# Two-block transformer kernel: the first norm's squares made between the copies of x and added by VectorE

## The reference, cut to what matters

```python
def rms_norm(x, gain):
    xf = x.astype(jnp.float32)
    xf = xf * lax.rsqrt(jnp.mean(xf * xf, axis=-1, keepdims=True) + NORM_EPS)
    return (xf * gain.astype(jnp.float32)).astype(x.dtype)
...
for l in range(DEPTH):                       # DEPTH = 2
    h = rms_norm(x, norm_mix[l])
    proj = h @ w_in[l]                       # 1024 -> 5120 columns
    ...                                      # two attentions, gates, output projection
    x = x + mixed @ w_out[l]
    h = rms_norm(x, norm_ffn[l])
    x = x + conv_ffn(h, w_up[l], conv_w[l], conv_b[l], w_down[l])
return rms_norm(x, norm_final)
```

## Time and profile before

| | |
|---|---|
| median of 3 runs | 1078.23 us (1077.58 to 1080.33) |
| the profiled execution | 1077.55 us, its span 1075.5 us |
| TensorE busy | 1057.4 us, 98% of the span |
| VectorE / ScalarE / GpSimd busy | 717.1 / 572.3 / 289.2 us |
| mean granted clock of TensorE | 0.996 |

### The profile page before, as it was taken

One profiled execution on the slowest core, in us unless ns is written; L12 is line 12 of the kernel. 1 busy time (PEld: TensorE's weight loads), 2 busy tenths in 40 slices (PEclk: granted clock), 3 DMA queues, 4 the chain that ended last, 5 costly groups with the idle time before them and its releaser, 6 DMA issues.

```text
span 1075.5 us, 20022 instructions
## 1 busy us (share of the span) xinstructions
PE 1057.4 (98%) x8402; PEld 1004.7 (93%) x8402; DVE 717.1 (67%) x1209; ACT 572.3 (53%) x789; POOL 289.2 (27%) x186
## 2 busy tenths in 40 slices
PE   7999999999999999999999999999999999999997
PEld 6999998999899899999999989998999999999996
DVE  3772228788678766322688867877887789666663
ACT  4545356564355553653756544556557865343442
POOL 2176675300000127566750000003300034101020
PEclk9899999999999999999999999999999999999999
DMA  8454444555664575344455557537333157564751
GB/s 293 157 184 131 157 155 159 165 188 170 218 197 142 182 230 178 105 150 157 134 182 195 187 170 230 167 123 212 116 113 118 60 177 225 172 212 130 242 176 39
DMA packets 169689, 180.11 MB, mean 167 GB/s; under 512 B 4224, under 2 KB 166400, under 8 KB 169472
## 3 DMA queue, kind: packets, MB, share of 16 engines
q1 hardware_dynamic: 169600, 178.84, 51.8%
HBM read 177.78 MB, written 1.05 MB: 166 GB/s over the span
## 4 chain that ended last, share of the span: by engine, by line
PE 90%; DVE 3%; ACT 3%; POOL 2%; issue 1%; DMA 1%; SPq 0%; DVEq 0%; POOLq 0%; ACTq 0%
PE psum L669 89%; ACT sb_scratch L1311 1%; DVE sb_w_lo L1824 1%; DMA sb_raw<-in_w_in 1%; ACT sb_w_hi L1311 1%; POOL sb_w_lo L2565 1%; POOL sb_rs L2581 1%; PE psum L888 1%; DVE psum L1815 0%; DVE sb_xg_lo L1815 0%; ACT sb_xg_hi L1311 0%; POOL sb_scratch L2603 0%; ACT sb_sq L1311 0%; DVE sb_scratch L1815 0%; ACT L1311 0%
## 5 line engine op out<-in xcount | busy, mean ns | idle before, releaser
L669 PE MATMUL psum<-sb_xg_hi,sb_w_hi 128*128 128x256 f32 x1656 | 411.3, 286 | 1.0 <-DVE sb_xg_lo L1815 1.0
L1311 ACT ACTIVATE sb_w_hi<-sb_raw 128x2048 fp32r<-128x2048 f32 (+3 forms) x185 | 318.1, 1724 | 176.7 <-PE psum L669 113.2
L669 PE MATMUL psum<-sb_xg_lo,sb_w_hi 128*128 128x256 f32 x1656 | 406.2, 283 | 0.0
L1824 DVE TENSOR_TENSOR sb_w_lo<-sb_raw,sb_w_hi 128x2048 fp32r<-128x2048 f32 (+3 forms) x151 | 307.1, 2037 | 114.7 <-ACT sb_w_hi L1311 113.9
L669 PEld LDWEIGHTS psum<-sb_xg_hi,sb_w_hi 128*128 128x128 f32 x1656 | 316.9, 191 | 4.0 <-DVE sb_xg_lo L1815 1.5
L669 PEld LDWEIGHTS psum<-sb_xg_lo,sb_w_hi 128*128 128x128 f32 x1656 | 317.4, 192 | 0.3
L669 PE MATMUL psum<-sb_xg_hi,sb_w_lo 128*128 128x256 f32 x1656 | 234.6, 285 | 0.7 <-DVE sb_w_lo L1824 0.7
L669 PEld LDWEIGHTS psum<-sb_xg_hi,sb_w_lo 128*128 128x128 f32 x1656 | 214.5, 192 | 1.6 <-DVE sb_w_lo L1824 0.9
L669 PE MATMUL psum<-sb_hid_both,sb_w_hi 128*128 128x512 f32 (+1 forms) x912 | 210.4, 364 | 1.2 <-DVE sb_hid_both L1899 1.2
L2565 POOL TENSOR_TENSOR sb_w_lo<-sb_raw,sb_w_hi 128x2048 fp32r<-128x2048 f32 (+1 forms) x34 | 156.1, 4597 | 111.1 <-ACT sb_w_hi L1311 101.2
L669 PEld LDWEIGHTS psum<-sb_hid_both,sb_w_hi 128*128 128x128 f32 x912 | 150.4, 190 | 22.6 <-DVE sb_hid_both L1899 2.5
(11 more groups left out here) (168 smaller groups left out, 997.1 us busy)
## 6 DMA issues: line engine op xcount, KB each, us to landing
sb_raw<-in_w_in SPq DMA_DIRECT2D x52, 1024.0 KB, 5.2
sb_raw<-in_w_up SPq DMA_DIRECT2D x44, 1024.0 KB, 5.1
sb_raw<-in_w_ff SPq DMA_DIRECT2D x21, 1024.0 KB, 5.8
sb_raw<-in_w_down SPq DMA_DIRECT2D x16, 768.0 KB, 4.8
sb_raw<-in_w_down SPq DMA_DIRECT2D x16, 640.0 KB, 4.4
sb_raw<-in_w_out SPq DMA_DIRECT2D x8, 1024.0 KB, 5.2
sb_raw<-in_w_ff SPq DMA_DIRECT2D x8, 768.0 KB, 4.5
sb_raw<-in_w_ff SPq DMA_DIRECT2D x8, 640.0 KB, 4.5
```

Of the source, the lines that this page charges most:

```text
L669: return nc.tensor.matmul(ps, lhsT, rhs, start=start, stop=stop, skip_group_check=True)
L1311: return nc.scalar.activation(out_, in_, func, **kw)
L1824: v.tensor_tensor(part(w_lo, s), part(raw, s), part(w_hi, s).bitcast(F32), ALU.subtract)\
```

## The change

ScalarE makes the squares of tiles 0 to 3 right behind the fourth `xg_full`, before the fifth, and those of tiles 4 to 7 at the old place. `sq` now has four buffers for them (`m % 4`). The additions move from GpSimd to VectorE: three of them behind the copies of x tiles 4, 5 and 6, the other four behind the low half of slab 1 and ahead of the low half of slab 2. ScalarE's split of slab 2 stays behind the last square. The counts of the semaphores are kept in step.

```diff
+            def first_square(m):
+                f(tl(sq, m % 4), tl(xt, m), ACT.Square).then_inc(S["square"], 1)
...
                 f(tl(xg_full, m), tl(xt, m), ACT.Copy, scale=col("norm_mix0", m)).then_inc(S["xg_full"], q.one("xg_full"))
+                if m == 3:
+                    for i in range(4):
+                        first_square(i)
                 if m == 4:
                     split(1)
...
-            for m in range(KD):
-                q.next("x_tile")
-                square_room(m)
-                f(tl(sq, m % 2), tl(xt, m), ACT.Square).then_inc(S["square"], 1)
+            for m in range(4, KD):
+                act.wait_ge(S["sq_added"], max(m - 4, 1))
+                first_square(m)
+            q.next("x_tile", KD)
+            q.next("sq_added", KD - 1)
+            q.next("stat_sum")
             split(2)
...
+            def add_square(m):
+                dve.wait_ge(S["square"], m + 1)
+                if m > 1:
+                    dve.wait_ge(S["sq_added"], m - 1)
+                v.tensor_tensor(SUMS[0], tl(sq, 0) if m == 1 else SUMS[0], tl(sq, m % 4), ALU.add).then_inc(S["sq_added"], 1)
...
             for m in range(KD):
                 if q.due("x_turned", m + 1):
                     dve.wait_ge(S["x_turned"], m + 1)
                 v.tensor_copy(tl(xt, m), turned(m)).then_inc(S["x_tile"], 1)
+                if 4 <= m < 7:
+                    add_square(m - 3)
...
             split(1)
+            for m in range(4, KD):
+                add_square(m)
             split(2)
...
-            add_squares()
+            q.next("square", KD)
+            q.next("stat_sum")
+            q.sent["sq_added"] = KD - 1
```

## The result

The changed kernel takes 1071.84 us, the median of 4 runs (1071.60 to 1072.89), against 1078.10 us for the kernel before. The ratio is 0.9938, with a 95% interval of 0.9922 to 0.9954. Five more runs on another occasion gave 1072.10 against 1078.20 us and 0.9944 [0.9931, 0.9958]; one execution of the kernel before took 5334.77 us there and is left out of the ratio. The prediction was 1071.8 us.

What follows compares the result with a forecast made beforehand. TensorE, busy 98% of the span, was taken to bound the kernel. Pause 4.4 plus clock 2.0 minus 0.2 us at slab 8 gave 6.2 us gained: 1071.8 us, own range 1070.8 to 1072.8, wider range 1070.5 to 1074.2.

Steps and rivals of the forecast that it cites:

- The pause, 4.4 us: TensorE's wait ahead of the first norm's stat() goes: stat() at 23.7 us against 28.09, 4.4 us gained.
- The clock, 2.0 us: TensorE's matmuls from 28.09 to 32.53 us, run at 1.2 GHz, would keep 2.4 GHz: 2.0 us gained.
- full clock: Profile reading that TensorE, busy 352.41 of 353.00 us from 30 to 383 us, ran at 2.4 GHz throughout.
- Squares and early additions at nothing: In the opening, ScalarE's first four squares (1.33 us) and VectorE's first three additions (0.45 us each) fit idle time: no cost.
- a sign of being wrong: In the profile after, a copy of x later than before would count against the prediction.
- The late additions, 1.8 us: VectorE's last four additions behind slab 1's low half, one every 0.45 us, complete the sum at 23.6 to 23.7 us.
- at the same moment: The sum of squares is ready just when TensorE, done with 8 low matmuls, could start stat(), at 23.71 us.
- Slab 2: ScalarE splits it at 20.3 us instead of 26.66, VectorE's low half runs 23.65 to 25.9: 1.1 us of slack for TensorE.
- Minus 0.2 us at slab 8: Other engines gain 4.95 us against TensorE's 6.4; 1.4 us less slack makes VectorE 0.2 us late for TensorE's sb_b.
- the short pause that stays: Rival: additions before stat() at GpSimd's pace leave a 1.6 us pause; gain 4.6 us, 1073.6 us, chance 0.10.
- the thin slack at slab 8: Rival: slack elsewhere is thinner than read, TensorE takes on all of 1.4 us; gain 5.0 us, 1073.2 us, chance 0.06.
- the first rival: Additions before stat() slow, one every 0.87 us, four in 3.5 us: a 1.6 us pause, 1073.6 us, chance 0.10.

Runs made afterwards that it cites:

- fill_pause: Kernel before with 32 extra matmuls on TensorE ahead of stat(), inside its pause, into an unused bank; 1076.34 us, ratio 0.9987.
- more_turns: Changed kernel with 22 instead of 16 idle turns on TensorE before x has landed; 1073.55 us, ratio 0.9950.
- hold_slab2: Changed kernel, but ScalarE waits for stat() before it splits slab 2; 1075.39 us, ratio 0.9971.
- pad_vector: Changed kernel with four extra dependent additions on VectorE behind the low half of slab 2, result unused; 1073.03 us, ratio 0.9957.
- low_first: Changed kernel with VectorE's low half of slab 2 ahead of the last four additions instead of behind them; 1075.68 us, ratio 0.9979.
- late_squares: Changed kernel with all eight squares back behind the xg_hi tiles and all seven additions on VectorE behind slab 1's low half; 1074.47 us, ratio 0.9964.
- gpsimd_adds: Changed kernel with all seven additions back on GpSimd, squares still early and in four buffers; 1075.98 us, ratio 0.9981.

## Why the prediction was right, step by step

- **The pause, 4.4 us.** 5.34 us from the low pass to `stat()` became 0.96: 4.38 us. Against the second profile of the kernel before it is 4.49 - 0.96 = 3.5 us. fill_pause, which keeps the pause and only its clock, was 4.2 us slower than the changed kernel (1076.34 - 1072.10), so the split between pause and clock holds in the medians too.
- **The clock, 2.0 us.** 4.44 us became 2.34: 2.1 us. In the second profile of the kernel before it was 1.4 us by the same rows, and against fill_pause it is 1.7 and 1.0. So 2.0 us lies near the upper end of what the profiles show. The prediction's "full clock" over the window from 30 to 383 us is a rounded mean: its first 2.5 us were at half, which changes 1.00 by less than 0.004.
- **Squares and early additions at nothing.** 1.32 us for four squares (1.33 was said), 0.69 us of ScalarE's idle time left behind them and 0.33 us left between the copies. In the first profile x was copied later than before, which the prediction had named as a sign of being wrong; the rows above show neither in its way, and the twelve low passes are no later with them.
- **The late additions, 1.8 us.** They took 2.01 us; a dependent addition comes every 0.53 us, not 0.45. It cost nothing, since TensorE came later to `stat()` in all three profiles of the changed kernel than in the first of before. With TensorE at 22.99 us, in more_turns, the sum is late by 0.15 us: the prediction's "at the same moment" was optimistic by about that.
- **Slab 2.** Its high half starts at 20.62 us (20.3 was said) and its low half at 24.07 (23.65). TensorE met both without waiting. hold_slab2 shows that the step was needed.
- **Minus 0.2 us at slab 8.** The place is the narrowest (pad_vector). The loss was nothing in the first and third profile of the changed kernel, where VectorE still waited 0.18 and 0.28 us for ScalarE, and 0.27 us in the second, where `sb_b` took 2.31 us instead of 2.04:

```profile
68.22 2.31 PE L669 MATMUL psum<-sb_scratch,sb_consts 128*128 128x256 f32 x12
```

- **The rivals.** None came true in this kernel, but two of them were made to: the short pause that stays (low_first, late_squares) and the thin slack at slab 8 (pad_vector). The 0.87 us that the first rival takes from GpSimd's additions holds only outside VectorE's subtractions; beside them it is 2.6 us.
- **The scatter.** The prediction allowed that the 2.0 us would vary between executions of the kernel before and that the changed kernel's own runs would scatter less. That came true. On one occasion 20 runs of the kernel before lay between 1076.84 us (mean granted clock 0.998) and 1080.52 us (0.994). The nine runs of the changed kernel lie between 1071.60 and 1072.89 us, all at 0.997 to 0.999, and the eleven of fill_pause between 1076.04 and 1077.86 us at 0.997 to 0.999. So about half of the spread goes when the pause is only filled (3.7 us become 1.8). Where the clock fell in the longest runs no profile shows.
- **The sum, and the luck in it.** 6.2 us was said, and the medians give 6.3 and 6.1 us. The profiles give less. The prediction started from the profile with the earliest low pass of all twelve (22.75 us), and so from the longest pause. It put the new `stat()` at 23.7 us; it came at 24.69, 24.31 and 24.91. L888 was at 104.74 and 104.61 us and is at 99.21, 99.08 and 99.42: 5.4 us earlier in the mean. The two first profiles differ by 1077.55 - 1071.93 = 5.6 us. The medians make up for it since the typical run of the kernel before is slower than both of its profiles (1078.2 against 1077.55 and 1077.41), by the scatter above. The mechanism was right; that the sum fits to 0.1 us is partly luck.

What stays open: why the clock falls in one pause of 2.4 us and not in another. In the opening it fell in seven of the twelve profiles, behind waits for x of about 1.6 to 2.2 us, and stayed up behind others of 1.9 us.

## What to carry to other kernels

A pause of the bounding engine is worth more than its length if its clock falls in it. Here it was 3.5 to 4.4 us of pause and 1.4 to 2.1 us of slow matmuls behind, and filling the pause with idle matmuls alone gives the second part. When a reduction is taken off the path, what stands behind it in the other engines' queues has to move as well: without the early split of the next slab two fifths to a half of the gain are lost. Once the wait is gone, look where the next engine's slack is thinnest; 1.8 us of extra work on VectorE now cost 1.3, at a place where the kernel before had 1.23 us of idle time.

## What the runs showed of the hardware that was not expected

- GpSimd's addition of two 128x256 tiles takes 0.73 us alone and 2.60 to 2.85 us (five of them, in four profiles) beside VectorE's two-input subtractions of 128x2048, and VectorE pays as well: two of them took 5.58 us instead of 4.6.
- Two kernels with a pause of TensorE of 2.4 us at the same place: in gpsimd_adds the granted clock was 0.50 behind it (28 to 30 us), in low_first it stayed at 1.00. The difference is 1.6 us from the low pass to L888.
- The dependent additions on VectorE, each of which also has a wait for its square, came every 0.53 us (2.01 us for four), while two dependent operations without such a wait took 0.88 us, one every 0.45 us. The four additions put into pad_vector, of the same shape and with only the wait for the one before, came every 0.46 us:

```profile
26.25 1.80 DVE L1963 TENSOR_TENSOR sb_rs<-sb_xt 128x256 f32<-128x256 f32 x4
```

So it is not the operation. The second wait is the likely cause; but these four also read x and not the running sum, so it is not shown apart.
